# Projection of the encoder layer: head mean and rotation at fixed lags behind the product, rotated halves stored each by itself into a scratch laid out by half, then head

## The reference

```python
xn = rms_norm(x, norm_mix)
q, k, v, u, g_attn, g_ssm = split(xn @ w_in)       # 1024, 256, 256, 512, 1024, 1024 columns
q = apply_axial_rope(rms_norm(q, q_norm))          # 16 heads of 64
k = apply_axial_rope(rms_norm(k, k_norm))          # 4 heads of 64
attn_out = gqa_attention(q, k, v) @ w_attn_proj
y = gelu(s5_bidirectional(u, ...)); ssm_out = (y @ w_glu_a) * sigmoid(y @ w_glu_b)
x = x + (sigmoid(g_attn) * attn_out + sigmoid(g_ssm) * ssm_out) @ w_out
x = x + square(relu(rms_norm(x, norm_mlp) @ w_ff1)) @ w_ff2
```

## Time and profile before

| | |
|---|---|
| time, median of 3 runs (lowest, highest) | 2879.03 us (2878.75, 2879.97) |
| the profiled execution: its time, its span | 2883.3 us, 2881.5 us |
| mean granted TensorE clock over the span | 0.956 |
| busy over the span: PE, DVE, POOL, ACT | 2634.2, 1635.7, 1555.1, 931.7 us |
| last product of `project` ends | 443.2 us |
| `gates_and_states`, `attention`, `tail` begin about | 449, 892, 1440 us |

### The profile page before, as it was taken

The page is one execution under the profiler, slowest core; times in us unless marked ns, Lnnn a source line. Parts: engine busy times, 40 slices in busy tenths (PEclk is TensorE's granted clock), DMA queues, the critical chain, the costliest instruction groups (busy, mean ns, idle before and its releaser), DMA issues.

```text
span 2881.5 us, 39384 instructions
## 1 busy us (share of the span) xinstructions
PE 2634.2 (91%) x11302; PEld 2101.0 (73%) x11302; DVE 1635.7 (57%) x1821; ACT 931.7 (32%) x1311; POOL 1555.1 (54%) x1237
## 2 busy tenths in 40 slices
PE   7777687887885999999799999999999999999999
PEld 4555566776774667777588888878888888888887
DVE  6444425577564999999656733535654343563441
ACT  4322211111111544444434322333433223442331
POOL 3111175776773789999744544444444444444444
PEclk9988888998997999999999999999999999999999
DMA  4111121222226321111352223454223245322223
GB/s 157 59 64 64 71 110 62 62 80 62 61 65 143 75 52 44 44 44 44 102 167 99 95 95 100 134 171 143 95 95 100 97 147 178 120 95 96 101 95 117
DMA packets 150416, 274.13 MB, mean 95 GB/s; under 512 B 51784, under 2 KB 64712, under 8 KB 150216
## 3 DMA queue, kind: packets, MB, share of 16 engines
q1 hardware_dynamic: 150344, 273.19, 29.9%
HBM read 222.16 MB, written 48.76 MB: 94 GB/s over the span
## 4 chain that ended last, share of the span: by engine, by line
PE 49%; DMA 1%; POOL 0%; DVE 0%; ACT 0%; issue 0%; SPq 0%; DVEq 0%; POOLq 0%; ACTq 0%
PE t_ps L62 16%; PE t_ps L64 16%; PE t_ps L63 16%; DMA t_wraw<-w_tail_t 1%; POOL t_wlo L1633 0%; DMA t_x<-mix_scratch 0%; DVE t_hlo L1743 0%; ACT t_whi L1647 0%; DVE t_x L1807 0%; PE t_ps L1841 0%; SPq L1606 0%; ACT t_hhi L1653 0%; SPq L1539 0%; SPq L1566 0%; SPq L1549 0%
## 5 line engine op out<-in xcount | busy, mean ns | idle before, releaser
L1633 POOL TENSOR_TENSOR t_wlo<-t_wraw,t_whi 128x1024 fp32r<-128x1024 f32 x266 | 671.1, 2523 | 794.3 <-ACT t_whi L1647 794.3
L1249 POOL TENSOR_TENSOR a_plo<-a_p,a_phi 128x512 fp32r<-128x512 f32 x320 | 452.7, 1441 | 60.0 <-DVE a_phi L1337 60.0
L1647 ACT ACTIVATE t_whi<-t_wraw 128x1024 fp32r<-128x1024 f32 x266 | 281.5, 1058 | 619.9 <-PE t_ps L64 553.6
L62 PE MATMUL t_ps<-t_hhi,t_whi 128*128 128x512 f32 x960 | 374.7, 390 | 0.0
L62 PE MATMUL t_ps<-t_ahi,t_whi 128*128 128x512 f32 x960 | 373.7, 389 | 0.5 <-POOL t_wlo L1633 0.5
L64 PE MATMUL t_ps<-t_hhi,t_wlo 128*128 128x512 f32 x960 | 373.5, 389 | 0.0
L63 PE MATMUL t_ps<-t_alo,t_whi 128*128 128x512 f32 x960 | 373.5, 389 | 0.0
L64 PE MATMUL t_ps<-t_ahi,t_wlo 128*128 128x512 f32 x960 | 373.5, 389 | 0.0
L63 PE MATMUL t_ps<-t_hlo,t_whi 128*128 128x512 f32 x960 | 373.4, 389 | 0.0
L1337 DVE CAST a_phi<-a_p 128x512 fp32r<-128x512 f32 x320 | 259.6, 818 | 42.0 <-ACT a_p L1280 39.8
L1807 DVE TENSOR_TENSOR t_x<-t_ps,t_x 128x512 f32 (+1 forms) x96 | 66.4, 691 | 373.6 <-PE t_ps L64 373.6
(11 more groups left out here) (203 smaller groups left out, 4793.0 us busy)
## 6 DMA issues: line engine op xcount, KB each, us to landing
t_wraw<-w_tail_t SPq DMA_DIRECT2D x266, 512.0 KB, 3.2
w_raw<-w_in_t SPq DMA_DIRECT2D x32, 512.0 KB, 4.8
proj_scratch<-stage SPq DMA_DIRECT2D x48, 256.0 KB, 2.0
a_q<-roped_scratch SPq DMA_DIRECT2D x48, 256.0 KB, 3.0
t_graw<-proj_scratch SPq DMA_DIRECT2D x24, 512.0 KB, 4.7
roped_scratch<-p_r_hi SPq DMA_DIRECT2D x30, 256.0 KB
roped_scratch<-p_r_lo SPq DMA_DIRECT2D x30, 256.0 KB
t_graw<-mix_scratch SPq DMA_DIRECT2D x14, 512.0 KB, 4.3
```

The lines of the kernel that those rows point to most:

```text
L62: pe.matmul(out, whi, xhi, start=start, stop=False)
L1249: pool.tensor_tensor(p_lo[s][:], p32[s][:], f32(p_hi[s][:]), ALU.subtract).then_inc(plo_done, 1)
L1633: pool.tensor_tensor(w_lo[s][:], w_raw[s][:], f32(w_hi[s][:]), ALU.subtract).then_inc(wlo_ready, 1)
L1647: act.activation(w_hi[s][:], w_raw[s][:], ACT.Copy).then_inc(whi_ready, 1)
```

## The change

What it does, part by part:

- **Stores.** `roped` is laid out `[half, head, 64, tokens]` where it was `[head, half, 64, tokens]`. Each half goes out in a DMA of its own, over 128 plain rows (two heads of 64), with its own semaphore (`hi_out`, `lo_out`): the high half once ACT has made it, the low half once DVE has. `r_hi` no longer waits for the low half's store.
- **Lags.** Head mean 2 places behind the product (`MEAN_LAG`), rotation 3 (`ROPE_LAG`), low half 4 (`LO_LAG`). The low half of the product before is computed between DVE's cos multiply and its sum.
- **Weights.** ACT's `high` waits for the product just done; DVE's `low` stands after `r` = 2 and 5.
- **Start.** Block 2 of x is loaded at once into `stage` and `r_hi`, as 8 DMAs. All splits come before all squares' sums; the first two `x_means` come after product 4, the third after product 5; evictions wait for all three norms. The first six head means go out two at a time, after products 6 to 8.
- **Attention.** A head of q is read by three DMAs of 64 rows (was two, of 128 and 64).
- One semaphore serves for the `turn` increments of all stages, which nothing waits for.

```diff
@@ project @@
+        slots = [sh.slot[b][:].rearrange("p (k n) -> p k n", k=KD) for b in range(2)]
+        late = [stage[i % 2][:, i // 2 * BLK:(i // 2 + 1) * BLK] for i in (0, 2, 1, 3, 4, 5)]
+        late += [f32(r_hi[:, i]) for i in range(2)]
+        x_tile = lambda b, k: slots[b][:, k] if b < 2 else late[k]
...
-        MEAN_LAG = 5
+        MEAN_LAG, ROPE_LAG, LO_LAG = 2, 3, 4
+        def means_due(i, r):
+            if is_first(i):
+                return (0, 1) if r == 5 else ()
+            if isinstance(i, int) and i == 1 and r < 2:
+                return (2 * r - 4, 2 * r - 3)
+            return (r - MEAN_LAG,)
...
@@ SP @@
+                for j in range(4):
+                    load_late(j)
...
                 def pair(i, behind, own):
-                    for s in range(2):
-                        sp.wait_ge(wlo_ready, 2 * i + (s + 1))
-                        load_w(2 * i + s + 2, s)
-                        if behind:
-                            for b in range(NBLK):
-                                r = 3 * s + b - 6
-                                sp.wait_ge(lo_ready, 6 * i + (r + 1))
-                                for l, part in enumerate((r_hi, r_lo)):
-                                    sp.dma_start(roped[bass.ds(4 * i + (2 * s - 4), 2), l, :, cols(b)],
-                                                 f32(part[:, r % 2])).then_inc(roped_out[r % 2], 16)
+                    for r in range(6):
+                        if r % NBLK == 0 and not is_first(i):
+                            s = r // NBLK
+                            sp.wait_ge(wlo_ready, 2 * i + (s + 1))
+                            load_w(2 * i + (s + 2), s)
+                        k = r - ROPE_LAG
+                        if has(i, k, behind, own):
+                            sp.wait_ge(hi_ready, 6 * i + (k + 1))
+                            rows, tok = place(i, k)
+                            sp.dma_start(rows_of(0)[rows, tok], f32(r_hi[:, k % 2])).then_inc(hi_out[k % 2], 16)
+                        k = r - LO_LAG
+                        if has(i, k, behind, own):
+                            sp.wait_ge(lo_ready, 6 * i + (k + 1))
+                            rows, tok = place(i, k)
+                            sp.dma_start(rows_of(1)[rows, tok], f32(r_lo[:, k % 2])).then_inc(lo_out[k % 2], 16)
...
@@ ACT, pair @@
                     for r in range(6):
+                        if r in (2, 5):
+                            act.wait_ge(summed, 6 * i + (r + 1))
+                            high(r // NBLK, 16 * i + 32)
...
-                        k = r - 1
+                        k = r - MEAN_LAG
...
-                        k = r - 2
+                        k = r - ROPE_LAG
                         if has(i, k, behind, own):
                             act.wait_ge(sum_ready, 6 * i + (k + 1))
                             if not first or k >= 2:
-                                act.wait_ge(roped_out[k % 2], 96 * i + 32 * (k // 2))
+                                act.wait_ge(hi_out[k % 2], 48 * i + 16 * (k // 2))
                             act.activation(r_hi[:, k % 2], qn[:, k % 2], ACT.Copy).then_inc(hi_ready, 1)
-                        if r == 2:
-                            act.wait_ge(summed, 6 * i + 6)
-                            high(1, 16 * i + 32)
-                        if r == 5 and not last:
-                            act.wait_ge(summed, 6 * i + 9)
-                            high(0, 16 * i + 48)
...
@@ DVE, pair @@
-                        if has(i, r - 2, behind, own):
-                            rope(i, r - 2, kinds[int(r >= 2)])
-                        if b == 0:
+                        if first and r == 2:
+                            low(s, 2 * i + (s + 3))
+                        k = r - ROPE_LAG
+                        if has(i, k, behind, own):
+                            rope(i, k, kinds[int(k >= 0)])
+                        if has(i, k - 1, behind, own):
+                            low_half(i, k - 1)
+                        if has(i, k, behind, own):
+                            rope_sum(i, k)
+                        if b == 2 and not (first and r == 2):
                             low(s, 2 * i + (s + 3))
...
@@ attention, SP @@
-                    sp.dma_start(f32(q1[kv][:]), both[head][:, tok]).then_inc(q_in[kv], 16)
-                    sp.dma_start(f32(q2[kv][0:HEAD]), both[head][0:HEAD, tok]).then_inc(q_in[kv], 16)
+                    hi, lo = roped[0][head][:, tok], roped[1][head][:, tok]
+                    sp.dma_start(f32(q1[kv][0:HEAD]), hi).then_inc(q_in[kv], 16)
+                    sp.dma_start(f32(q1[kv][HEAD:P]), lo).then_inc(q_in[kv], 16)
+                    sp.dma_start(f32(q2[kv][0:HEAD]), hi).then_inc(q_in[kv], 16)
...
@@ encoder_layer @@
-    roped = scratch("roped_scratch", [NQ + NKV, 2, HEAD, TOK])
+    roped = scratch("roped_scratch", [2, NQ + NKV, HEAD, TOK])
```

More of the change, by code:

```diff
@@ L346, in _ @@
                         split(b, k)
[L347 to L350, removed]
                     if b == 1:
-                        for k in range(ACT_SQ):
-                            square(b, k)
+                        high(1, 16)
+                for b in range(2):
+                    for k in range(ACT_SQ):
+                        square(b, k)
+                act.wait_ge(x_mean, 1)
                 for k in range(ACT_SQ):
                     square(2, k)
-                act.wait_ge(summed, 3)
-                high(0, 32)
                 for b in range(NBLK):
@@ L366, in pair @@
                 def pair(i, behind, own):
-                    first, last = is_first(i), isinstance(i, int) and i == PAIRS_ - 1
+                    first = is_first(i)
                     if behind and not own:
@@ L544, in _, with low_half @@
                 dve.wait_ge(rope_in, 48)
-                def rope(i, r, kind):
-                    n, s, tok = 6 * i, r % 2, cols(r % 3)
-                    early = is_first(i) and r < 2
-                    dve.wait_ge(hrs_ready, n + (r + 1))
+                def low_half(i, k):
+                    n = 6 * i
+                    dve.wait_ge(hi_ready, n + (k + 1))
+                    if not (is_first(i) and k < 2):
+                        dve.wait_ge(lo_out[k % 2], 48 * i + 16 * (k // 2))
+                    dve.tensor_tensor(r_lo[:, k % 2], qn[:, k % 2], f32(r_hi[:, k % 2]),
+                                      ALU.subtract).then_inc(lo_ready, 1)
@@ L551, in rope @@
+                def rope(i, k, kind):
+                    n, s, tok = 6 * i, k % 2, cols(k % 3)
+                    early = is_first(i) and k < 2
+                    dve.wait_ge(hrs_ready, n + (k + 1))
                     if not early:
[L552 to L553 removed]
+                        dve.wait_ge(lo_ready, n + (k - 1))
+                    dve.scalar_tensor_tensor(qn[:, s], stage[k % 6 // 3][:, tok], head_gain[:, kind:kind + 1],
@@ L608, in _ @@
                 angles()
-                with dve.Fori(1, K_T // 2) as i:
+                pair(1, True, True)
+                with dve.Fori(2, K_T // 2) as i:
                     pair(i, True, True)
@@ L653, in pair @@
                         mm.then_inc(summed, 1)
-                        if first and r in (1, 2, 4):
-                            x_means((1, 2, 4).index(r))
-                        if has(i, r - MEAN_LAG, behind, own):
-                            if first:
-                                pe.wait_ge(rope_in, 48)
-                            head_mean(i, r - MEAN_LAG)
+                        if first and r == 3:
+                            x_means(0)
+                            x_means(1)
+                        if first and r == 4:
+                            x_means(2)
+                        for k in means_due(i, r):
+                            if has(i, k, behind, own):
+                                if first:
+                                    pe.wait_ge(rope_in, 48)
+                                head_mean(i, k)
                 all_pairs(pe, pair)
```

100 lines of the change are left out of this document (52 added, 48 removed).

## The result

| | before | changed |
|---|---|---|
| time, median (lowest, highest), 4 runs each | 2879.5 (2878.75, 2882.42) us | 2754.12 (2752.67, 2755.71) us |
| profiled execution: time, span | 2883.3, 2881.5 us | 2755.5, 2753.8 us |
| last product of `project` ends | 443.2 us | 316.7 us |
| from there to the first product of the gates | 6.0 us | 4.1 us |
| gates' first product to attention's first matmul | 452.9 us | 453.7 us |

The ratio is 0.9559 (95% interval 0.9547 to 0.9571): 4.4% less. In the spans, 126.5 of the 127.7 us come out of `project`, 1.9 out of the step behind it, and the later stages differ by less than 1 us each.

A forecast was written before the change was run, and what follows sets the result against it. The stores' rate was taken to bound `project`, with PE, DVE and ACT only waiting. 2883.3 - 128.8 (`project`) + 1.0 (attention) = 2755.5, by the median 2751 us; range 2741 to 2778.

The forecast's parts named there:

- The argument from 5.14 us per half to 10.28 per product: Stores of `project`: 256 KB halves at 51 GB/s take 5.14 us each, 10.28 per product, which bounds the stage.
- an eighth or 0.6 us per store: Stores of `project`: 16 engines instead of 2 would cut 5.14 us to 0.6, leaving the sum as it is.
- PE's round: q and k products: a product with its head mean costs PE 6.32 us, the mean 0.88 of it.
- The loss of 112.6 us: Products 12 to 36 of `project`: 270.6 us less 25 x 6.32; 91.7 idle, the rest matmuls at lower clock.
- Rival A: q and k products: DVE or ACT becomes the bound, rounds 6.8 to 7.3 us, 2763 or 2777 us; 0.26 with D.
- B: Stores of `project` keep their rate, 10.28 us per product remain, 2858 us; chance 0.04.
- C: q and k products: fixed lags close a ring, a round would be 13 us, 2925 us; chance 0.02.
- D: POOL's preparation, 16 us longer than before, ends last: some 5 to 10 us more; 0.26 together with Rival A.
- DVE's round: q and k products: 5.34 us, or 6.03 if the low half waits for POOL; 6.03 taken, hidden under PE's 6.32.
- The start: Start of `project`: splits end at 35.7 us, product 7 at 65.8 against 72.57, 6.8 saved.
- The tight place after the first pair: Behind the first pair of products DVE starts about 15 us behind; 1 us allowed.
- the sum's -127.8: Whole kernel: 128.8 us saved by product 48, 1.0 added in attention, from 2883.3 to 2755.5 us.

The follow-up runs named there:

- the second trace: The changed kernel run once more, unedited, as a yardstick beside the follow-up runs: 2754.08 us, ratio 0.9565.

## Why the prediction was right

**The bound and its removal.** The argument from 5.14 us per half to 10.28 per product holds from both sides: with the shape alone the round falls to 6.74, and with all the rest but the shape it stays at 10.62. Taken was 2.0 us for a store's landing; measured 2.0 and 2.3. The Trainium skill ("DMA: Bandwidth & Descriptors", section "Why a DMA increments its semaphore by 16 and not by 1") has the engines follow from what divides the slowest dimension of both sides. The runs agree: 2 rows of 64x512 gave 51 GB/s in either kernel, 64 or 128 plain rows did not. My estimate from that rule, an eighth or 0.6 us per store, no run shows; a landing took 2.0.

**PE's round.** 6.32 forecast, 6.31 measured, at clock 1.00. (The loss of 112.6 us counts a head mean behind product 36, which has none; it is 113.5. Nothing else rests on it.) Rival A (DVE or ACT the bound) didn't come: DVE waits 0.97 for PE where no weight part stands ahead. Rivals B and C are excluded by the 2.0 us and by the means at 6.31, D by POOL's idle 20.56 us.

**DVE's round: 6.03 was too much, it is 5.58.** The mechanism was right (1.78 us recorded, 1.9 expected if POOL blocks it), the size not. I added the whole 0.69 to the round. Shuffle to sum went from 2.72 us to 3.08 (150.20 to 153.28), 0.36 more. Behind the sum, in the experiment, the low half cost its own 0.6: 5.44 against 5.20 for the round. A likely reason for the rest is that the low half goes on with POOL's end itself, while the sum had to wait for the hand-over from POOL as well; that wasn't tried. It cost nothing, as PE hid either value. The Trainium skill ("SBUF — State Buffer", section "Who interferes with whom") states the exclusion; the trace agrees with 1.78 against 0.69 us, and shows that such an instruction adds only 0.36 us where the next one waits for POOL's result anyway.

**The start.** Splits 35.7 forecast, 35.6 measured; product 3: 36.3 and 36.8; 4: 41.8 and 42.3; 5: 50.8 and 51.2; 6: 58.6 and 59.2; 7: 65.8 and 66.4. The saving at product 7 was 6.3 us (the head mean behind it starts at 66.28, 72.57 before), not 6.8. The reason "ten of the 24 splits; with the four sums out of the way it would be fourteen" held too: sixteen splits end at 29.2, so fourteen by 27.8, and with the sums back the last split comes at 38.28. By that reason the order is worth four splits, 2.7 us; the 6 us that I expected of the experiment took the sums' own length for their cost. The other 3 to 4 us belong to what wasn't tried by itself. One part can be seen: in the kernel before, block 2's splits stood behind block 1's sums and beside POOL's squares, five of them in

```profile
39.27 6.23 DVE L520 SCALAR_TENSOR_TENSOR x_lo<-slot,p_gain,x_hi 128x512 fp32r<-128x512 f32 x5
```

1.25 us each, against 0.68 now. The places of `x_means` and of the first head means are the rest. That the early load of block 2 saves nothing itself was right.

**The tight place after the first pair.** 1 us allowed, 0.45 + 1.78 = 2.23 measured; moving the angles takes the 1.78 away and leaves the 0.45. This and the 0.6 at product 7 make most of the miss at the last product: 314.4 forecast, 316.7 measured.

**The stages behind.** POOL's last rotation: about 236 forecast, 237.5 measured; its preparation's end 298 and 300.7. Attention was to cost 1 us, and costs nothing that can be told (528.6 and, in the second trace, 527.5, against 528.1). Not foreseen: the step to the gates is 1.9 us shorter. There the last store of `project` is issued 0.9 us behind the last product, at 317.57, where it was 3.6, at 446.72; DVE's low part of the next weights now stands behind that eviction. So the sum's -127.8 meets the spans' -127.7 by luck, through two small misses of opposite sign, 2.3 us more in `project` and 2.2 less behind it. Of the medians, 2751 forecast and 2754.1 measured, the 3 us are the profiled executions' distance from the medians: 4.3 us over that of the kernel before, as I had it then, and 1.4 over that of the changed one.

## What to carry to other kernels

When an engine waits for another in a ring, follow the waits until a DMA issue that takes microseconds, and divide bytes by rate there: the store's outermost dimension of 2 was worth 107 us of 125, while new lags without it brought under 5. Lags pay only after the slowest link is gone, and the next bound then has to be looked up anew (here PE, 0.7 us over DVE). A layout that makes stores plain rows can turn a load of the other side into the bad shape; split that load, since one more issue was hidden and the bad shape cost 55 us.

## What the runs showed of the hardware

- A 2x64x512 access is dear for loads as well as for stores. One such load per head, 256 KB, made attention 50 us longer, though it is one DMA fewer.
- Two stores of 64 rows and one of 128 rows are equal (2772.8 and 2774.2 us), at 1.13 us of issue for the two against 0.33 for one.
- DVE's subtraction is recorded at 1.78 us beside a POOL multiplication, and 0.69 alone, but lengthens the round by less than 0.4 us, so the recorded time of a blocked instruction here overstates its cost.
- TensorE's granted clock between 20 and 30 us (1.00 is 2.4 GHz, 0.5 is 1.2, what lies between a mix of the two) is 0.62 in the kernel before and 0.63 with block 0's sums among its splits, and 1.00 in the changed kernel, where the splits come without sums between them and PE had run products for 8.57 of the 12 us ahead (8 to 20 us), not 5.83 and 5.60. In the two kernels with 0.62 and 0.63 the clock had already fallen within those 12 us, to 0.89 and 0.88 on average.
